# A transformer pair on one core: X parked in DRAM behind the experts, and another order of attention work on VectorE

## The reference, cut to what matters

```python
def _layer(x, ctx, ...):          # the first block
    h = modulate(rmsnorm(x))
    mixed = w_out(gates * (neighbourhood_attention(h) , ssd(h)))   # "the mixer"
    x = x + gate * rmsnorm(mixed)
    h2 = modulate(rmsnorm(x))
    # experts: 16, each takes its 64 best tokens of 512 (expert choice)
    #   y = (silu(t @ w_gate) * (t @ w_up)) @ w_down,  1024 -> 2048 -> 1024
    x = x + gate * rmsnorm(sum of the experts' outputs at their tokens)

for layer in range(2):            # the second kind
    h = rms_norm(x, g_mix[layer])
    # heads 0-3: differential attention (two score maps a head, a = p0 - lam * p1)
    # heads 4-7 and 8-15: causal attention with other masks, one map a head
    x = x + concat(o_a, o_b, o_c) @ w_out[layer]
    x = x + conv_gated_mlp(rms_norm(x, g_ffn[layer]))
return rms_norm(x, g_final)
```

## Time and profile before

| | |
|---|---|
| runs, median of 3 | 3853.85 us (3851.75 to 3857.58) |
| the profiled execution | 3861.44 us, span 3859.6 us |
| TensorE products busy | 3611.0 us, 94% of the span |
| VectorE, ScalarE, GpSimd busy | 1152.5, 763.5, 427.5 us |
| granted TensorE clock, mean | 0.985 |
| moved by DMA | 634.08 MB, mean 164 GB/s |
| neighbourhood attention | about 579 to 884 us of the span |
| X and router | about 1200 to 1292 us |
| experts | 1296 to 2262 us |
| attention of the two second layers | about 2302 to 2590 and 3085 to 3375 us |

### The profile page before, as it was taken

How to read it: one execution, slowest core, us unless ns; L and a number is a source line. 1 busy time by engine, 2 the same in 40 slices (tenths; PEclk the granted TensorE clock), 3 DMA queues, 4 the chain that set the end, 5 groups by cost and what they waited for, 6 DMA issues and landing times.

```text
span 3859.6 us, 33017 instructions
## 1 busy us (share of the span) xinstructions
PE 3611.0 (94%) x12600; PEld 1742.4 (45%) x12600; DVE 1152.5 (30%) x2612; ACT 763.5 (20%) x1772; POOL 427.5 (11%) x393
## 2 busy tenths in 40 slices
PE   7999999999999888888887889999999999999999
PEld 3555555454444433323332344555444545554444
DVE  3356666243101303100111035443220144432211
ACT  2135554223102101000000022222110122221100
POOL 0003334021000000000000002101220021012200
PEclk9899999999999899999999999999999999999999
DMA  8423333112124699999999961012221211122120
GB/s 280 162 67 93 93 93 90 45 57 82 66 87 170 262 409 409 409 409 409 409 409 409 409 229 55 33 55 87 66 87 66 78 53 39 39 93 87 66 82 28
DMA packets 302209, 634.08 MB, mean 164 GB/s; under 512 B 32554, under 2 KB 145818, under 8 KB 301798
## 3 DMA queue, kind: packets, MB, share of 16 engines
q1 hardware_dynamic: 241278, 592.28, 41.0%
q10 hardware_dynamic: 60776, 39.70, 3.9%
HBM read 625.50 MB, written 10.24 MB: 165 GB/s over the span
## 4 chain that ended last, share of the span: by engine, by line
PE 73%; DMA 18%; DVE 4%; SPq 1%; ACT 1%; issue 1%; POOL 1%; DVEq 0%; POOLq 0%; ACTq 0%
PE psum L308 31%; PE psum L1642 9%; DMA arena<-in_w_exp_gate_dram 7%; DMA arena<-in_w_exp_up_dram 7%; PE psum L810 6%; PE psum L2445 4%; PE psum L2902 4%; PE psum L2938 4%; DMA arena<-in_w_exp_down_dram 4%; PE psum L1466 2%; PE psum L1494 2%; PE psum L1475 2%; PE psum L2923 1%; SPq L277 1%; PE psum L2371 1%
## 5 line engine op out<-in xcount | busy, mean ns | idle before, releaser
L308 PE MATMUL psum<-arena 128*128 128x512 f32 (+1 forms) x3200 | 1301.3, 565 | 2.6 <-POOL arena L2044 2.4
L308 PEld LDWEIGHTS psum<-arena 128*128 128x128 f32 x3200 | 608.1, 192 | 675.4 <-issue 653.4
L2445 PE MATMUL psum<-arena 128*64 128x512 f32 x3072 | 692.9, 596 | 143.9 <-DMA arena<-in_w_exp_up_dram 74.4
L2445 PEld LDWEIGHTS psum<-arena 128*64 128x64 f32 x3072 | 232.8, 136 | 585.2 <-issue 566.7
L1642 PE MATMUL psum<-arena 128*128 128x512 f32 x768 | 344.3, 602 | 0.0
L810 PE MATMUL psum<-arena 128*128 128x512 f32 (+1 forms) x768 | 256.2, 491 | 1.1 <-DVE arena L550 1.1
L1642 PEld LDWEIGHTS psum<-arena 128*128 128x128 f32 x768 | 144.3, 191 | 187.1 <-issue 186.2
L2981 POOL TENSOR_SCALAR arena<-arena 128x512 f32<-128x512 f32 x88 | 138.3, 1572 | 687.4 <-ACT arena L2960 687.4
L1574 DVE CUSTOM_DVE_ANT_0 arena<-psum,arena 128x512 f32<-128x512 f32 (+3 forms) x224 | 113.7, 545 | 302.2 <-PE psum L1466 302.2
L2987 DVE SCALAR_TENSOR_TENSOR arena<-arena 128x512 f32<-128x512 f32 x88 | 66.3, 753 | 426.4 <-POOL arena L2981 426.4
L810 PEld LDWEIGHTS psum<-arena 128*128 128x128 f32 x768 | 144.6, 191 | 107.9 <-issue 96.3
(11 more groups left out here) (276 smaller groups left out, 2885.2 us busy)
## 6 DMA issues: line engine op xcount, KB each, us to landing
arena<-in_w_exp_gate_dram SPq DMA_DIRECT2D x128, 1024.0 KB, 18.6
arena<-in_w_exp_up_dram SPq DMA_DIRECT2D x128, 1024.0 KB, 18.5
arena<-in_w_exp_down_dram SPq DMA_DIRECT2D x128, 1024.0 KB, 18.7
arena<-in_w_in_dram SPq DMA_DIRECT2D x64, 1024.0 KB, 5.2
arena<-in_w_up_dram SPq DMA_DIRECT2D x88, 512.0 KB, 4.8
arena<-in_w_ada_dram SPq DMA_DIRECT2D x24, 1024.0 KB, 9.1
arena<-in_w_down_dram SPq DMA_DIRECT2D x20, 1024.0 KB, 5.1
arena<-acs_scratch ACTq DMA_DIRECT2D x64, 256.0 KB, 6.0
```

Source lines behind the costliest of these rows:

```text
L308: mm = pe.matmul(shaped(b, l, r), l, r, start=kt == 0, stop=kt == nkt - 1)
L2445: mm = pe.matmul(banks[n][64 * j:64 * j + 64, :], lhs[:, kt, 64 * j:64 * j + 64], w, start=kt == 0, stop=kt == 2 * nkb - 1)
```

## The change

It has three parts. First, each tile of X is written to a DRAM tensor `xD` as soon as its norm has been applied (`act_out1`), and read back near the end of the last pair of experts (`act_X_back`), when the last but one weight block has landed; GpSimd and VectorE wait for it before they add. Second, the memory of X (two slots) and that of the mixer's `mix` (one slot) take three more blocks of the first pair, so that blocks 13 to 19 go to places that are used once and the ring of 13 takes over at block 20 instead of 17. Blocks 15 and 16 now go where X was and wait for its store; blocks 17 and 18 wait as 15 and 16 did; block 19 waits for the router's last transposition. Third, in `dve_att_2` the order of the parts within a step changes, for all three attentions, and the reciprocals move from the step after into the unit's own step. Some semaphores are merged under one name (`con_in`, `gain_in`, `X_io`).

```diff
-            yield from att2_steps(J, (1, sums), (1, weights), (0, scores), (2, turned), (3, outs), (4, heads))
+            yield from att2_steps(J, (1, weights), (2, turned), (0, scores), (0, sums), (3, outs), (4, heads))
...
-        W.bufs += [sb(SB + 2048, WSLOT), sb(BASE + 4096, WSLOT), sb(SB + 11264, WSLOT), sb(SB + 11264 + WSLOT, WSLOT)]
+        W.bufs += [sb(SB + 2048, WSLOT), sb(BASE + 4096, WSLOT), sb(SB + 11264, WSLOT), sb(SB + 11264 + WSLOT, WSLOT),
+                   sb(BASE, WSLOT), sb(BASE + WSLOT, WSLOT), sb(SB + 9216, WSLOT)]
...
+        xD = dram("X_scratch", [128, 4, 1024])
...
                 act_tile_rows(act, "r1", X, i, h2)
+                act.dma_start(xD[:, i, :], X[:, i, :]).then_inc(*up(S("X_io"), *([("X_out",)] if i == 3 else []), by=16))
...
             elif n == 15:
+                sp.wait_ge(*at("X_out"))
+                wait_all(sp, [("xn", "r1", 3, 0), ("xn", "r1", 3, 1)])
+                slots[:] = [NW + 12, NW + 13]
+            elif n == 17:
                 sp.wait_ge(*at("full", ("h2", 3, 1)))
                 slots[:] = [NW + 10, NW + 11]
-            elif n == 17:
+            elif n == 19:
+                sp.wait_ge(*at("full", "slot"))
+                slots[:] = [NW + 14]
+            elif n == 20:
                 slots[:] = range(NW + 8)
+
+        def act_X_back(act):
+
+            for key in ((("e", 0, 0, "u", 1), 3), (("e", 0, 1, "g", 0), 0), (("d", 7, 0), 7)):
+                act.wait_ge(*at("wfull" if key[0][1] else "wfree", key))
+            for i in range(4):
+                act.dma_start(X[:, i, :], xD[:, i, :]).then_inc(*up(S(f"x_in{i}"), ("X_back", i), by=16))
...
+            if m == 7:
+                act_X_back(act)
...
                         if i == 3:
+                            if h == 0:
+                                dve.wait_ge(*at("X_back", i))
...
             for i in range(3):
+                pool.wait_ge(*at("X_back", i))
```

More of the change, by code:

```diff
@@ L1280, in act_finish @@
                 if t == 11:
-                    act.dma_start(dcon, dsrc).then_inc(*up(S("dcon_in"), ("dcon",), by=16))
+                    act.dma_start(dcon, dsrc).then_inc(*up(S("con_in"), ("dcon",), by=16))
                 act.dma_start(yD[:, t, :], yTb[t % 2]).then_inc(*up(S(f"y_out{t % 2}"), ("yD", t), by=16))
@@ L2085, in act_out1 @@
             act.wait_ge(*at("branch_end"))
-            act.dma_start(X, xT).then_inc(*up(S("X_in"), ("X_in",), by=16))
+            act.dma_start(X, xT).then_inc(*up(S("X_io"), ("X_in",), by=16))
             for k in range(4):
                 act.wait_ge(*at("gam", 2 if k < 2 else 5, k % 2))
-            act.dma_start(gam1, gamD[0:1, :].rearrange("a n -> (a n)").partition_broadcast(128)).then_inc(*up(S("gam1_in"), ("gam1",), by=16))
+            act.dma_start(gam1, gamD[0:1, :].rearrange("a n -> (a n)").partition_broadcast(128)).then_inc(*up(S("gain_in"), ("gam1",), by=16))
             act.dma_start(iota, fsrc).then_inc(*up(S("iota_in"), ("iota",), by=16))
@@ L2496, in act_experts @@
             if m == 6:
-                act.dma_start(gam2, gamD[1:2, :].rearrange("a n -> (a n)").partition_broadcast(128)).then_inc(*up(S("gam2_in"), ("gam2",), by=16))
+                act.dma_start(gam2, gamD[1:2, :].rearrange("a n -> (a n)").partition_broadcast(128)).then_inc(*up(S("gain_in"), ("gam2",), by=16))
+            if m == 7:
+                act_X_back(act)
             for n in range(1 if m == 7 else 2):
@@ L2549, in act_moe_end @@
         def act_moe_end(act):
-            act.dma_start(gcon, gsrc).then_inc(*up(S("gcon_in"), ("gcon",), by=16))
+            act.dma_start(gcon, gsrc).then_inc(*up(S("con_in"), ("gcon",), by=16))
             act.preload_act_table_set(LNEXP)
@@ L3163, in act_program @@
                     act.wait_ge(*at("attn_end", L))
-                    act.dma_start(gf, A["g_final"].partition_broadcast(128)).then_inc(*up(S("gf_in"), ("gf",), by=16))
+                    act.dma_start(gf, A["g_final"].partition_broadcast(128)).then_inc(*up(S("gain_in"), ("gf",), by=16))
                 act_mlp(act, L)
```

## The result

| | median (range) | runs |
|---|---|---|
| before, same chip | 3854.05 us (3851.75 to 3857.58) | 4 |
| after | 3827.97 us (3826.08 to 3828.70) | 4 |

The ratio is 0.9926, with a 95% interval of 0.9913 to 0.9938: the change saves 24 to 34 us by the ratio and 26.1 by the medians. The forecast was 11.7 us. The profiled execution took 3828.7 us, its span is 3826.7.

The account below looks back on a forecast made before the run. TensorE was taken to bound the kernel nearly everywhere and the weight stream the expert stage. Experts 6.6, first attention 3.3 and later attentions 1.8 summed to 11.7 us: 3842 us on the median, range 3830 to 3850.

Parts of the forecast that it names:

- What bounds the kernel: Whole kernel: TensorE sets the pace nearly everywhere, busy 94% of the span; the weight stream sets it in the expert stage.
- Three more blocks early: Expert weight stream: three more blocks fit into idle DMA time before the first product, 3 x 2.56 = 7.7 us off.
- Pause at block 33: Expert stream: block 33 waits for blocks 20 and 21 to be read; 1.1 us lost, 6.6 us left.
- Storing X and loading it back: X's store before the experts and load near their end: costs nothing, with 7 us in hand for tile 0.
- Rival C: End of the experts: X lands behind six projection loads, 12 us after its need; 3854, no change; chance 0.05.
- First attention: First attention: three waits for the bank that the copy frees shrink or go, saving 3.3 us.
- The two later attentions: Each later attention: 1.1 + 1.0 - 0.6 - 0.6 = 0.9 us saved by VectorE's new order, both 1.8.
- Four small bank waits go: 1.1: Each later attention: TensorE's waits of 0.18, 0.26, 0.34 and 0.34 us go, saving 1.1 us.
- The GpSimd conflict: Later attentions: GpSimd's scaling delays VectorE's rotation product by 0.9 to 1 us, turning 0.6 to -0.4, 0.3 to -0.2.
- Rival A: All three attentions: all TensorE waits on VectorE go, 36 us, 3818; half of them, 3832; chance 0.12.
- Rival B: Attentions: TensorE sees the new wait for exponentials, 0.9 us per step, 43 us; 3887, a third 3858; chance 0.08.
- Rival D: Expert stream: gives only 1 to 2 us, through a longer pause or a later one; 3847; chance 0.10.

Follow-up runs that it names:

- e6: Changed kernel with the old VectorE order and 17 early blocks in their old places, all X traffic kept; 3854.62 us, ratio 0.9994.
- e12: The changed kernel timed once more, on another chip; 3825.41 us, ratio 0.9930.
- e7: Kernel before with six PSUM banks for attention and two for fillers instead of five and three, old order, no X part; 3842.97 us, ratio 0.9963.
- e9: Changed kernel with early reciprocals for differential units only, and GpSimd's scaling of those written with two tensor inputs; 3816.96 us, ratio 0.9909.
- e4: Kernel before with only the reciprocals moved, right behind the unit's own score bias, the turned tile's copy staying behind them; 3901.45 us, ratio 1.0127.
- e3: Kernel before with only the copy of the turned tile moved ahead of the score bias; 3828.21 us, ratio 0.9942.
- e8: Kernel before with one more early block, in the place of mix, X untouched, old order; 3852.63 us, ratio 0.9991.
- e2: Changed kernel with the old VectorE order, so the X part with 20 early blocks alone; 3851.09 us, ratio 0.9996.

## Why the prediction was wrong, point by point

- **What bounds the kernel:** right. TensorE nearly everywhere, the weight stream in the experts.
- **Three more blocks early, 7.7 us:** right in mechanism; the issue at 1292.78 shows it.
- **Pause at block 33, 1.1 us:** in the right place, sized too small. It took 2.8 us of stream, inside my bounds (0 to 3.65). I had taken the two landing times as if the queue were full up to the one and at full rate from the other on. Net 5.7 us (4.9 to 6.8) for a term of 6.6.
- **Storing X and loading it back, 0:** right, e6. Tile 0 had 7.7 us in hand, where I had 7. Rival C is refuted, as the loads landed in 6.4 to 10.2 us beside a full weight queue.
- **First attention, 3.3 us:** right in size by some luck. From its first to its last score it gave 4.5 us, up to the experts 3.9; in e12, with less low clock, 6.1 and 5.5. Each of the two waits of 1.41 us cost 1.64, the fourth wait (925.29), outside the window that I had read, gave as much again, and the wait for the output bank (L1606) was 2.3 us where my walk had left 1.5, with 16 filler products at the low clock behind it (8.83 us in place of 7.13).
- **The two later attentions, 0.9 us each: the step that failed.** They gave 8.8 and 10.3 us. The sizes were wrong, and one term had the wrong sign (the next point). "Four small bank waits go: 1.1" was the larger error: three of them alone cost 3.65 us, since a wait between the two maps' products takes away their overlap, which e7 shows by itself. The clock, which the sum had at nothing, goes with 4.4 us of gain in this half in the profiled execution, before 2.1 us are given back at a longer wait for weights. The same kind of error put a pair of tail waits at 2.46 us, where it held up 2.85, and gave the new wait in the tail no price for the clock behind it. I had priced each wait by what stands in its brackets.
- **The GpSimd conflict, 0.6 turned to -0.4 and 0.3 to -0.2:** wrong. Beside the one-input scaling the product isn't slowed at all. VectorE's way from the start of the scores to the end of the next weights became 5.72 us (2355.20 to 2360.92) from 6.52 (2371.10 to 2377.62), a gain of 0.8, and 0.3 at the second place: near the 0.6 and 0.3 that I had before the conflict was put in. The row that I took as nearest was of another operation of GpSimd. The rule of the Trainium skill that I set beside it ("SBUF — State Buffer", section "SBUF: two separate sides": an exclusive lock for the whole instruction) isn't borne out by this trace for the one-input scaling when that began first (0.69 us under cover of 1.57). It agrees better the other way round, where VectorE began first and the scaling took 1.30 us in place of 0.93. For the two-input one, e9's product lost 0.30 of the 0.44 us that they overlapped.
- **Rival A** (half of the waits go, 3832) gives nearly the right time for the wrong reason: the listed waits of the later attentions fell by 1.9 and 2.7 us, not by half. **Rival B** is what e4 is, and it doesn't happen where the copy stands ahead of the reciprocals. **Rival D** is refuted by the 5.7 us that the profiles show in the stream.
- **What I said would make it wrong,** a change of TensorE's waits on VectorE by over 5 us a layer, didn't occur. The view that I would have tested it by was the one that misled me.

What stays open: e3 and e7 show the banks as the common cause, and e7 the price of the lost overlap at two of the waits. The rest of the split of a later attention's gain, between clock and later arrival, is read from aligned timelines of one profiled execution each; how much of the low clock is due to the waits, and how much differs from one execution to the next, no kernel here separates.

## What to carry to other kernels

Price a wait of TensorE by the distance between the same products with and without it, not by its idle time: look at whether the instructions on both sides of it run side by side elsewhere in the trace, and whether the filler behind it runs at the low clock. When two uses of one in-order engine compete, put first the one that frees a bank and last the one that itself waits for another engine; of the two parts of this order the first gave 22 us, and the second without the first cost 49. An operation's slowdown beside another engine holds for the pair that the row shows; take it over only for the same form of both and the same one in front. And read an attention's waits over the whole of it: find its first and last product in the trace first.

## What the hardware showed that I had not expected

- Score products of two maps, on different rows of the array, overlap fully: four in 0.70 us, two in 0.69 (256 keys). A wait of 0.18 us between them costs 0.87.
- The stretch ahead of the first attention, the same code in all kernels, took 649.5 to 662.5 us, by when the granted clock fell to 1.2 GHz. In the window from 170 to 180 us e8 (649.5) had the full clock where the kernel before (662.5) had half of it; the column ahead of the DMA share is the clock:

```profile
170.00:180.00 10.00, 10.00 (x73) 8.47 (x73) 2.65 (x6) 1.54 (x2) 0.00 (x0) 1.00 0.53 183
```

```profile
170.00:180.00 10.00, 10.00 (x48) 10.00 (x49) 2.72 (x4) 0.96 (x1) 0.00 (x0) 0.50 0.51 188
```

Both kept TensorE busy for all 10 us, one with 73 products and one with 48. This alone puts up to 13 us between two profiled executions, more than the whole X part. It can hide a shorter expert stage in the runs of e2 and e8; that it did isn't shown, since the other runs weren't profiled.
